# Sums of squared residuals on GpSimd, and a new order of the weight splits in the norm

## The chip, the core and the metric

The kernel runs on one core of one Trainium2 chip, as one program. The metric is the device time of one execution in microseconds (us), from its start to its end. The profile is of one execution of the same program.

## The reference

The program computes one sequence of 256 tokens with 1024 features through two blocks. The first is a Mamba-2 mixer and a convolutional feed-forward net, then an attention with dilated windows and a second such net. The second has two layers, each with a retention and convolution mixer, a cross-attention to a memory, and a gated net. What bears on the change is that every sub-layer starts with an RMS norm of the running sum x and ends by adding its output to x:

```python
def rms_norm(x, g):
    xf = x.astype(jnp.float32)
    y = xf * lax.rsqrt(jnp.mean(xf * xf, axis=-1, keepdims=True) + RMS_EPS)
    return (y * g.astype(jnp.float32)).astype(x.dtype)

# first block
x = x + _mamba2_mixer(_rms_norm(x, a_norm[i]), ...)
x = x + _conv_ffn(_rms_norm(x, ffn_norm[layer]), ...)
x = x + _dilated_mixer(_rms_norm(x, b_norm[j]), k_sh, v_sh, ...)
# second block, for each layer
u = rms_norm(h, norm_mix_g[l])
h = h + mixer_sublayer(u, ...)
h = h + memory_cross_attention(rms_norm(h, norm_xattn_g[l]), mem_n, ...)
h = h + conv_ffn(rms_norm(h, norm_ffn_g[l]), w_up[l], ...)
```

## The kernel before

Activations lie with features on the 128 partitions: x is 8 chunks of 128 features by 256 tokens. All weights are streamed from HBM as 350 units of up to 128x2048 elements, four buffers `raw` deep. Products are made to float32 accuracy from three passes in the faster fp32r format: each weight unit and each input is split into a high part and a low part, and TensorE multiplies high by high, high by low and low by high. ScalarE casts `raw` into `w_hi` (its `split`, L2054; in halves L2051 and L2052 for a few units), VectorE subtracts it to make `w_lo` (its `split`, L1191; in halves L1186 and L1188). Both have two buffers, so unit g+2 can be cast only when TensorE is done with unit g. A "feat" unit is 2 chunks of output from 8 chunks of input: 48 matmuls of 256 columns into one PSUM bank, in the order of the semaphores `hi_ready`, `lo_ready`, `unit_done`, `acc_free`.

The units form segments (`up_a`, `down`, `att_k`, ...), which all engines walk through in the same order. On each engine the order of the work is written out by hand, one instruction queue for each engine, with `project` running a segment unit by unit: split of unit u+2, `first` (what empties the bank), `second` (what has time). SyncE issues the load of a unit when `lo_ready` says that its buffer's former unit has been split.

**The end of a sub-layer** is `residual` on VectorE. For the kind "feat" (att_o, mix of both layers, mem_o of both layers; 4 units each) each unit goes: x plus the bank for two chunks (L1321), then `early_parts`, which makes the un-normalised input x times the next norm's gain and splits it (in_hi L1278, in_lo L1282), then the split of unit u+2, then in `second` two additions `ssum += sq2[m]` (L1342). The squares `sq2` are made by ScalarE (L2130, in its own `residual`) once x is ready and the former two sums are done (`sum_ready`). The other kinds (ssm_out, down) work chunk by chunk, wholly on VectorE, and aren't touched.

**The start of a sub-layer.** The first three units of the next segment (EARLY = 3) multiply the un-normalised input, so they don't wait for the norm; their banks are multiplied by 1/rms afterwards (`scale_unit`, L1197). Meanwhile TensorE sums `ssum` over the partitions with one matmul (`norm_stats`, L769). It stands behind the whole of the segment's first unit for those behind a "feat" residual and for glu of layer 0, and behind half of it otherwise. ScalarE takes the root (L2089), VectorE the reciprocal (L1368), and `norm` on VectorE makes the normalised input: eight scalings `scaled` into xn (L1375), which ScalarE casts to in_hi in four pieces (`high_parts`, L2105) and VectorE subtracts to in_lo in four pieces (`low_parts`, L1385). Unit 3 is the first to use it. `norm` also holds the splits of the segment's units 2 and 3, placed by hand. It runs seven times: ffn_a(0), attention, ffn_a(1), mixer(0), ffn_b(0), mixer(1), ffn_b(1). The cross-attention (mem_q) has its own code instead. Behind `norm`, in the two kinds of ffn, VectorE runs the convolution's taps on unit 0 (L1625, L1628), then the split of unit 4, and so on (`behind=8`); in ffn_b a product (L1680) frees the unit's bank.

**GpSimd** holds the mask of the Mamba scan, the product L2664 (up_a only) and some in_lo parts (L2654, L2697). In the attention, cross-attention and mix segments its queue was empty (`skip`).

## Time and profile before

| what | us |
|---|---|
| median of 3 runs | 2103.97 (2103.52 to 2105.73) |
| the profiled execution, device time | 2104.84 |
| its span, first to last instruction | 2103.2 |
| TensorE busy, matmuls | 2073.7 (99%) |
| VectorE busy | 1666.5 (79%) |
| ScalarE busy | 1061.2 (50%) |
| GpSimd busy | 260.0 (12%) |

The mean granted TensorE clock is 0.998 of full speed. A busy TensorE still includes short waits, since the ends of its matmuls are modelled; the start of a unit against the end of the one before shows them better. In the trace an instruction's start is followed by its duration, and where its engine stood idle before it, by that time and what ended it.

### The profile page before, as it was taken

Reading aid. Unit: us, or ns where it says so; the run is one execution under the profiler, and the core shown is the slowest. Engines: PE = TensorE matmul, PEld = TensorE weight load, DVE = VectorE, ACT = ScalarE, POOL = GpSimd, SP = SyncE. Lnnn points to the kernel's source line nnn. Section 1 sums busy time; section 2 is a strip of 40 time slices with the busy share of each in tenths; the row PEclk is TensorE's granted clock in tenths of the full one; section 3 lists DMA queues with packets and bytes.
Section 4 is the critical chain, followed back from the end, with each engine's and each line's share of the span. In section 5 each row is a group of like instructions: output and inputs, shape, how many; then the busy total and the mean of one; then the engine's idle time right before and its main releaser. Section 6 shows DMA issues by size and latency. Waiting matters only on the chain.

```text
span 2103.2 us, 40039 instructions
## 1 busy us (share of the span) xinstructions
PE 2073.7 (99%) x16378; PEld 2015.8 (96%) x16378; DVE 1666.5 (79%) x2449; ACT 1061.2 (50%) x1282; POOL 260.0 (12%) x176
## 2 busy tenths in 40 slices
PE   9999999999999999999999999999999999999998
PEld 9999999999989999989999999999988999989998
DVE  8897888788778877898986768768698996758765
ACT  6886444357754434355545445444346445445442
POOL 0212055000005500001202001100000301100100
PEclk9999999999999999999999999999999999999999
DMA  6553545453335455453554444445453555534543
GB/s 261 191 194 131 187 181 183 165 214 141 121 116 185 156 184 208 169 179 142 199 182 181 160 142 173 180 159 208 181 181 141 182 186 182 176 137 166 189 150 117
DMA packets 58281, 361.66 MB, mean 172 GB/s; under 512 B 6736, under 2 KB 9360, under 8 KB 21136
## 3 DMA queue, kind: packets, MB, share of 16 engines
q1 hardware_dynamic: 58128, 359.48, 47.9%
q8 instruction: 113, 1.85, 0.4%
q14 instruction: 40, 0.33, 0.0%
HBM read 358.37 MB, written 1.08 MB: 171 GB/s over the span
## 4 chain that ended last, share of the span: by engine, by line
PE 88%; DVE 6%; ACT 2%; issue 2%; DMA 1%; POOL 1%; SPq 0%; DVEq 0%; ACTq 0%; POOLq 0%
PE acc L639 72%; PE acc L638 7%; DVE w_lo L1191 2%; ACT w_hi L2054 1%; PE acc L754 1%; PE acc L755 1%; PE acc L756 1%; DVE arena L1413 1%; PE acc L959 1%; PE pA L1008 0%; DVE arena L1456 0%; DMA raw<-in_wide 0%; PE pB L1032 0%; PE pD L1119 0%; PE pB L1119 0%
## 5 line engine op out<-in xcount | busy, mean ns | idle before, releaser
L639 PE MATMUL acc<-in_hi,w_hi 128*128 128x256 f32 x4656 | 1306.2, 286 | 16.9 <-issue 12.1
L639 PE MATMUL acc<-in_hi,w_lo 128*128 128x256 f32 x4656 | 1292.7, 283 | 0.1
L639 PE MATMUL acc<-in_lo,w_hi 128*128 128x256 f32 x4656 | 1230.2, 283 | 0.0
L2054 ACT CAST w_hi<-raw 128x2048 fp32r<-128x2048 f32 (+1 forms) x341 | 615.4, 1805 | 667.5 <-PE acc L639 587.0
L1191 DVE TENSOR_TENSOR w_lo<-raw,w_hi 128x2048 fp32r<-128x2048 f32 (+1 forms) x341 | 738.8, 2167 | 233.2 <-ACT w_hi L2054 231.6
L639 PEld LDWEIGHTS acc<-in_hi,w_hi 128*128 128x128 f32 x4656 | 891.8, 192 | 25.8 <-issue 22.4
L639 PEld LDWEIGHTS acc<-in_hi,w_lo 128*128 128x128 f32 x4656 | 891.9, 192 | 0.6 <-DVE w_lo L1522 0.3
L639 PEld LDWEIGHTS acc<-in_lo,w_hi 128*128 128x128 f32 x4656 | 854.9, 192 | 1.2 <-issue 1.0
L2654 POOL TENSOR_TENSOR in_lo<-arena,in_hi 128x256 f32 (+2 forms) x112 | 145.2, 1296 | 1217.7 <-ACT in_hi L2514 515.7
L1835 DVE SCALAR_TENSOR_TENSOR arena<-arena,cols 128x256 f32<-128x256 f32 x480 | 200.3, 487 | 0.0
L2664 POOL TENSOR_TENSOR arena<-arena 128x256 f32<-128x256 f32 x44 | 81.9, 1861 | 387.9 <-ACT arena L2336 387.9
L2338 ACT CAST in_hi<-arena 128x256 f32 (+1 forms) x88 | 35.8, 407 | 185.8 <-POOL arena L2664 99.3
L1628 DVE SCALAR_TENSOR_TENSOR arena<-acc,cols,arena 128x255 f32<-128x255 f32 (+1 forms) x264 | 114.8, 476 | 9.2 <-DVE arena L1628 2.0
L1625 DVE TENSOR_SCALAR arena<-acc,cols 128x256 f32<-128x256 f32 x132 | 62.1, 498 | 42.3 <-PE acc L639 38.0
L638 PE MATMUL acc<-w_hi,in_hi 128*128 128x512 f32 (+1 forms) x240 | 91.0, 382 | 0.0
L638 PE MATMUL acc<-w_lo,in_hi 128*128 128x512 f32 (+1 forms) x240 | 88.2, 370 | 0.0
L638 PE MATMUL acc<-w_hi,in_lo 128*128 128x512 f32 (+1 forms) x240 | 86.1, 369 | 0.0
L638 PEld LDWEIGHTS acc<-w_hi,in_hi 128*128 128x128 f32 x240 | 45.3, 189 | 7.9 <-issue 0.5
L638 PEld LDWEIGHTS acc<-w_lo,in_hi 128*128 128x128 f32 x240 | 45.2, 188 | 7.7
L638 PEld LDWEIGHTS acc<-w_hi,in_lo 128*128 128x128 f32 x240 | 44.3, 189 | 8.0 <-issue 1.0
L754 PE MATMUL acc<-in_hi,w_hi 128*128 128x256 f32 x160 | 46.2, 289 | 0.2
L755 PE MATMUL acc<-in_lo,w_hi 128*128 128x256 f32 x160 | 45.2, 283 | 0.0
(293 smaller groups left out, 1628.1 us busy)
## 6 DMA issues: line engine op xcount, KB each, us to landing
raw<-in_wide SPq DMA_DIRECT2D x285, 1024.0 KB, 4.8
raw<-in_narrow SPq DMA_DIRECT2D x64, 704.0 KB, 4.0
arena<-cs_rows SPq DMA_DIRECT2D x16, 256.0 KB, 4.6
arena<-in_mem SPq DMA_DIRECT2D x3, 1024.0 KB, 6.9
x<-in_x SPq DMA_DIRECT2D x4, 256.0 KB, 6.5
raw<-in_wide SPq DMA_DIRECT2D x2, 512.0 KB, 5.8
tables<-in_tables SPq DMA_DIRECT2D x1, 1024.0 KB, 15.4
arena<-cs_rows SPq DMA_DIRECT2D x16, 64.0 KB, 5.3
```

The lines of the kernel that those rows point to most:

```text
L638: return mm(outs[m], moving[:, c, at], w[:, k, :], start=start, stop=stop)
L639: return mm(outs[m], w[:, k, at], moving[:, c, :], start=start, stop=stop)
L754: mm(out, hi[:, k, at], in_hi[:, c, :], start=k == 0 and m == 0, stop=False)
L755: mm(out, hi[:, k, at], in_lo[:, c, :], start=False, stop=False)
L1191: tt(w_lo[g % 2][:, 0:n], raw[g % RAW][:, 0:n], w_hi[g % 2][:, 0:n], ALU.subtract).then_inc(lo_ready, 1)
L1625: E.mark(ts(out, bank, w(2), None, ALU.mult) if bias is None else ts(out, bank, w(2), bias, ALU.mult, ALU.add))
L1628: ins = stt(out=o, in0=bank[:, 0:T - n], scalar=w(2 - n), in1=o, op0=ALU.mult, op1=ALU.add)
L1835: ins = stt(out=cvo[:, c, :], in0=src, scalar=w, in1=cvo[:, c, :], op0=ALU.mult, op1=ALU.add)
L2054: copy(w_hi[g % 2][:, 0:n], raw[g % RAW][:, 0:n]).then_inc(hi_ready, 1)
L2338: copy(in_hi[:, bass.ds(u + DC, 1), :], f_h[:, r, :].unsqueeze(1)).then_inc(inh_ready, 1)
L2654: tt(in_lo[:, d, :], src(u, j), in_hi[:, d, :], ALU.subtract).then_inc(gin_ready, 1)
L2664: tt(f_h[:, j % 2, :], f_s[:, j % 2, :], f_v[:, j % 2, :], ALU.mult).then_inc(hid_ready, 1)
```

## The change

The change has two parts. First, the two additions a unit `ssum += sq2[m]` in the five "feat" residuals leave VectorE and stand in GpSimd's queue as `residual_sums`, in the attention, mixer and cross stages; VectorE no longer waits for the last sum at the end of such a residual. Second, `norm` on VectorE makes the splits of unit 2 and unit 3 earlier: unit 2's ahead of all eight scalings, and unit 3's directly behind the scaling of unit 0's bank, with all low parts and the scaling of unit 1's bank behind it. On ScalarE the cast of unit 3 stands between the second and the third high part.

```diff
--- before.py
+++ after.py
@@ -1335,12 +1335,7 @@
                 def second(u, j, banks):
                     if beside:
                         beside(u, j, banks)
-                    if kind == "feat":
-                        E.wait(square_a)
-                        for m in range(2):
-                            dve.wait_ge(sum_ready, u * 2 + (sums + 1 + m))
-                            tt(ssum, ssum, sq2[:, m, :], ALU.add).then_inc(sum_ready, 1)
-                    elif not (isinstance(u, int) and u == last):
+                    if kind != "feat" and not (isinstance(u, int) and u == last):
                         sums_of(u, j)
 
                 def sums_of(u, j):
@@ -1356,7 +1351,8 @@
                 seg = project(name, first_and_last, second, steps={v_order: marks}, early=kind == "feat")
                 E.passed(sum_ready, 1 + DC)
                 freed(seg)
-                dve.wait_ge(sum_ready, E.seen[sum_ready])
+                if kind != "feat":
+                    dve.wait_ge(sum_ready, E.seen[sum_ready])
                 return seg
 
             def squares(src, c):
@@ -1389,13 +1385,12 @@
 
                 seg, half = take.next(), NORM_PIECES // 2
                 reciprocal_std(rstd[:])
-                scaled(name, x, rstd, xn, val_ready, range(DC // 2))
                 split(2, seg, 2)
-                scaled(name, x, rstd, xn, val_ready, range(DC // 2, DC))
+                scaled(name, x, rstd, xn, val_ready)
                 scale_unit(seg, nth, 0)
+                split(3, seg, 3)
                 low_parts(xn, chunk0, half, DC // NORM_PIECES)
                 scale_unit(seg, nth, 1)
-                split(3, seg, 3)
                 low_parts(xn, chunk0, NORM_PIECES, DC // NORM_PIECES, first=half)
 
 
@@ -2098,8 +2093,8 @@
                 E.wait(ssum_ready)
                 root(pA[:, 0:T], 1.0 / D, "eps_rms", std_ready, std[:])
 
-            def high_parts(src, chunk0, pieces, each, ready=None):
-                for n in range(pieces):
+            def high_parts(src, chunk0, pieces, each, ready=None, first=0):
+                for n in range(first, pieces):
                     if ready is not None:
                         E.wait(ready)
                     copy(in_hi[:, slots(chunk0 + n * each, each), :], src[:, n * each:(n + 1) * each, :]
@@ -2109,9 +2104,11 @@
 
                 seg = take.next()
                 roots()
+                half = NORM_PIECES // 2
                 split(2, seg, 2)
-                high_parts(xn, chunk0, NORM_PIECES, DC // NORM_PIECES, val_ready)
+                high_parts(xn, chunk0, half, DC // NORM_PIECES, val_ready)
                 split(3, seg, 3)
+                high_parts(xn, chunk0, NORM_PIECES, DC // NORM_PIECES, val_ready, first=half)
 
             def two_roots():
 
@@ -2654,6 +2651,14 @@
                     tt(in_lo[:, d, :], src(u, j), in_hi[:, d, :], ALU.subtract).then_inc(gin_ready, 1)
                 E.sweep(seg, body)
 
+            def residual_sums(nth):
+
+                for u in range(DC // 2):
+                    E.wait(square_a)
+                    for m in range(2):
+                        pool.wait_ge(sum_ready, (1 + DC) * nth + 2 * u + 1 + m)
+                        tt(ssum, ssum, sq2[:, m, :], ALU.add).then_inc(sum_ready, 1)
+
             def ffn(name, n):
                 def multiply(u, j):
 
@@ -2680,7 +2685,18 @@
                     low_parts("conv_out", piece["mix"][l], lambda u: bass.ds(u * 2 + MIX_AT, 2),
                               lambda u, j: gate[:, bass.ds(u * 2 + DC, 2), :])
                     skip("mix")
+                    residual_sums(4 + 3 * l)
                 return run
+
+            def cross(l):
+                def run():
+                    skip("mem_q", "mem_v", "mem_o")
+                    residual_sums(5 + 3 * l)
+                return run
+
+            def attention():
+                skip("att_k", "att_v", "att_q", "att_o")
+                residual_sums(2)
 
             def ssd_mask(g):
 
@@ -2697,8 +2713,8 @@
                     tt(in_lo[:, d, :], xbc[:, 2 * g:2 * g + 2, :], in_hi[:, d, :], ALU.subtract).then_inc(gin_ready, 1)
                 skip("xbc", "z", "ssm_out")
 
-            stages(mamba, ffn("up_a", 0), lambda: skip("att_k", "att_v", "att_q", "att_o"),
-                   ffn("up_a", 1), second=lambda l: (mixer(l), lambda: skip("mem_q", "mem_v", "mem_o"),
+            stages(mamba, ffn("up_a", 0), attention,
+                   ffn("up_a", 1), second=lambda l: (mixer(l), cross(l),
                                                      ffn("up_b", 2 + l)))
```

## Rows read from the trace of the kernel before

**Rows 1.** The page, busy time of each engine: us (share of the span) xinstructions.

```profile
PE 2073.7 (99%) x16378; PEld 2015.8 (96%) x16378; DVE 1666.5 (79%) x2449; ACT 1061.2 (50%) x1282; POOL 260.0 (12%) x176
```

**Rows 2.** TensorE's waits over the whole span: us in total, times, longest us.

```profile
PE acc L639 <- issue: 12.1, 25, 1.1
...
PE acc L639 <- DVE in_hi L1278: 0.2, 1, 0.2
```

**Rows 3.** Timeline, end of att_o and start of ffn_a(1): start us, duration us, what.

```profile
605.46 2.28 DVE L1191 TENSOR_TENSOR w_lo<-raw,w_hi 128x2048 fp32r<-128x2048 f32 x1
...
607.84 0.35 PE L639 MATMUL acc<-in_hi,w_hi 128*128 128x256 f32 x1 [1.99 <-ACT w_hi L2054]
...
630.89 2.28 DVE L1191 TENSOR_TENSOR w_lo<-raw,w_hi 128x2048 fp32r<-128x2048 f32 x1
...
633.34 0.28 PE L639 MATMUL acc<-in_hi,w_hi 128*128 128x256 f32 x1
```

**Rows 4.** Timeline of the norm in ffn_b(0), VectorE and TensorE.

```profile
1264.88 1.67 DVE L1375 SCALAR_TENSOR_TENSOR arena<-x,cols,rstd 128x256 f32<-128x256 f32 x4
...
1268.86 0.35 PE L639 MATMUL acc<-in_hi,w_hi 128*128 128x256 f32 x1 [0.66 <-issue]
...
1270.86 1.28 DVE L1385 TENSOR_TENSOR in_lo<-arena,in_hi 128x512 fp32r<-128x512 f32 x2
...
1275.23 0.36 PE L639 MATMUL acc<-in_hi,w_hi 128*128 128x256 f32 x1 [0.39 <-issue]
...
1279.94 0.41 DVE L1680 TENSOR_TENSOR arena<-arena,acc 128x256 f32<-128x256 f32 x1
...
1281.06 0.28 PE L639 MATMUL acc<-in_hi,w_hi 128*128 128x256 f32 x1
```

**Rows 5.** The sums (L1342) and GpSimd's product (L2664): duration ns min/median/max.

```profile
L1342 DVE TENSOR_TENSOR arena<-arena x40: 412/422/427, 597.2 to 1905.3; 128x256 f32<-128x256 f32 x40
...
L2664 POOL TENSOR_TENSOR arena<-arena x44: 728/2369/2534, 262.8 to 742.0; 128x256 f32<-128x256 f32 x44
```

**Rows 6.** Timeline in ret_g of layer 0: VectorE and GpSimd side by side.

```profile
1021.61 1.26 DVE L1835 SCALAR_TENSOR_TENSOR arena<-arena,cols 128x256 f32<-128x256 f32 x3
...
1022.79 2.28 DVE L1191 TENSOR_TENSOR w_lo<-raw,w_hi 128x2048 fp32r<-128x2048 f32 x1
1022.89 3.33 POOL L2654 TENSOR_TENSOR in_lo<-arena,in_hi 128x512 fp32r<-128x512 f32 x1 [3.08 <-ACT in_hi L2514]
1025.00 2.30 DVE L1835 SCALAR_TENSOR_TENSOR arena<-arena,cols 128x256 f32<-128x256 f32 x3
```

**Rows 7.** Timeline, mix of layer 0 (first two) and the first unit behind mem_o.

```profile
1163.11 2.28 DVE L1191 TENSOR_TENSOR w_lo<-raw,w_hi 128x2048 fp32r<-128x2048 f32 x1
...
1165.56 0.29 PE L639 MATMUL acc<-in_hi,w_hi 128*128 128x256 f32 x1
...
1258.35 2.28 DVE L1191 TENSOR_TENSOR w_lo<-raw,w_hi 128x2048 fp32r<-128x2048 f32 x1
...
1261.86 0.38 PE L769 MATMUL pA<-arena,ones 128*128 128x256 f32 x1
```

**Rows 8.** Timeline of TensorE in mixer(0): the starts of units 2 and 4.

```profile
815.68 0.36 PE L639 MATMUL acc<-in_hi,w_hi 128*128 128x256 f32 x1 [0.56 <-issue]
...
827.87 0.28 PE L639 MATMUL acc<-in_hi,w_hi 128*128 128x256 f32 x1
```

**Rows 9.** Timeline in ffn_a(0): the split of unit 4 and its start.

```profile
261.25 2.28 DVE L1191 TENSOR_TENSOR w_lo<-raw,w_hi 128x2048 fp32r<-128x2048 f32 x1
...
264.20 0.28 PE L639 MATMUL acc<-in_hi,w_hi 128*128 128x256 f32 x1
```

**Rows 10.** Timeline in the attention's norm: VectorE, and TensorE at the second att_v unit.

```profile
448.65 0.69 DVE L1197 TENSOR_TENSOR acc<-acc,rstd 128x512 f32<-128x512 f32 x1
...
454.99 2.29 DVE L1191 TENSOR_TENSOR w_lo<-raw,w_hi 128x2048 fp32r<-128x2048 f32 x1 [1.46 <-ACT w_hi L2054]
...
458.13 0.28 PE L638 MATMUL acc<-w_hi,in_hi 128*128 128x256 f32 x1
```

## Prediction, made before the changed kernel was run

> **What bounds the kernel now.** I read the page's busy shares first [rows 1]: TensorE is busy for 99% of the span, so only what makes it wait can move the time. Next TensorE's list of waits: the longest entry is 25 short idles put down to "issue" in front of the weight products (L639), 12.1 us in all [rows 2]. In the timeline, the larger ones on which this change bears stand at a unit's start, right behind the VectorE subtraction that makes w_lo (L1191): 605.46 + 2.28 = 607.74, TensorE at 607.84 [rows 3], so the signal takes 0.10 us. In such places VectorE's queue is the bound; elsewhere it runs a little ahead of TensorE. So for each site I ask how much room there is, and whether the edit uses it up. A unit takes 5.8 us on TensorE (1275.23 to 1281.06 [rows 4]).
>
> **Part 1, sums on GpSimd.** In five residuals (att_o, mix twice, mem_o twice) VectorE loses two additions a unit, 40 in all, 0.42 us each [rows 5], which is 0.79 a unit in its queue, since neighbours overlap. GpSimd gains them. Its own two-operand instruction of this size takes 0.73 us at best, but 2.37 in the median [rows 5]. The timeline says why [rows 6]: a GpSimd subtraction (512 elements) that starts 0.10 us behind an L1191 ends 1.15 us after that L1191 (1022.89 + 3.33 against 1025.07), so it waited for it. It goes the other way too: three L1835, each with two operands in SBUF, take 1.26 us together before it, and 2.30 behind the L1191, where the first was issued while GpSimd was already waiting. So the two engines take turns, the one that asks first goes first, and GpSimd waits for no more than the instruction in flight.
>
> The Trainium skill ("SBUF — State Buffer", section "Who interferes with whom") has this as a rule: a VectorE instruction with two SBUF inputs contends with a GpSimd instruction that reads SBUF, and the one that issues first holds the shared ports for its whole length. The trace agrees, by the 2.30 against 1.26 us. By the rule rival 1 can't happen; without it part 1 would come to -1.6.
>
> What is left of a 256-element addition once VectorE lets go I take as 0.6 us (0.73 less its start), and its cost to a full VectorE queue as 0.55. In the residuals VectorE's in_lo products (L1282) and its splits (L1186, L1188, L1191) all read two SBUF tiles.
> - att_o (once): VectorE is full from the second unit's split up to the next segment's first, whose L1191 ends 0.10 before TensorE starts [rows 3]. Two pairs of sums gone ahead of it save 1.6; of GpSimd's six additions that ask before it five fall between VectorE's contending instructions, 0.55 each: 2.75. The first unit of up_a comes 1.15 later. There TensorE also waited for in_hi (L1278; an idle of 0.2 in the list [rows 2], 0.4 from start to start), which goes. Net +0.7. Bounds: -1.6 with no collision, +1.7 with six and nothing absorbed.
> - mix (twice): half of unit 2's split is held up 0.55, then unit 3's split as much, less the 0.8 of the sum that is gone: it ends 0.3 later. It ended at 1165.39, and TensorE came at 1165.56 [rows 7]; with the signal 0.07 is free: +0.23. In mem_o unit 3's split is further ahead: 0.
> - the last pair of sums (mix and mem_o, four times): TensorE reads ssum (L769) behind the next segment's first unit. VectorE's last split ends at 1258.35 + 2.28 = 1260.63; two additions on GpSimd (0.6, then 0.05 and 0.74) and a signal of 0.05 give 1262.07. L769 came at 1261.86 [rows 7]: +0.2. At best 0, at worst 1.6, with one addition behind a further instruction. In att_o the last square comes well before the split: nothing more.
>
> Sum of part 1: 0.7 + 2 x 0.23 + 4 x 0.2 = +2.0 us. ScalarE's next square now waits for GpSimd, and the next w_hi cast stands behind it; it is idle there in any case, waiting for TensorE. No DMA is moved; SyncE waits for lo_ready alone. GpSimd has nothing else to do then: it is busy 12% [rows 1], and its next work is the hidden layer's, later.
>
> **Part 2, the order in norm().** Seven norms. VectorE now does split(2) ahead of all eight scalings (before, behind four), and split(3) ahead of scale_unit(1) and all four low parts (before, behind the first three of these five). ScalarE casts unit 3's w_hi behind two high parts, not four. The work is the same; what counts is what now stands behind the splits. Four scalings take 1.6 us, two low parts 1.2 (1.28 with the overlap) [rows 4], a scale_unit 0.6 (0.69 [rows 10]): so 1.8 us move behind split(3).
> - ffn_b (twice): TensorE starts units 2 and 3 at 1268.86 and 1275.23, with idles of 0.66 and 0.39 shown; against its own 5.76 us a unit it is 0.82 and 0.55 late [rows 4]. Both waits go: 1.37. But split(3) starts only 1.6 us earlier and has 1.8 more behind it, so the taps, split(4) and the multiply that frees the bank (L1680, ending 1279.94 + 0.41 = 1280.35) come 0.25 later: 1280.6, with the signal 1280.7. TensorE used to start unit 4 at 1281.06. Of the 1.37 only this is kept: -0.37 each.
> - ffn_a(1): the same, but its taps are longer, and unit 4 at 633.34 stood right behind its split (630.89 + 2.28 = 633.17) [rows 3]. It now comes 0.17 later; the two gains before it are given back: +0.17.
> - mixer(0): the same two waits (0.56 shown at 815.68), and unit 4 began at 827.87 without a wait [rows 8]. The new limit is ScalarE, whose unit-1 function waits for scale_unit(1), and which casts unit 4 after it: about 822.9 to 824.8, the split to 827.2, TensorE 827.3: -0.6.
> - ffn_a(0): here the statistics come half a unit earlier and nothing waited. split(2) still waits for a cast that hangs on TensorE, so VectorE stands idle for the 1.6 us in which it used to scale. split(3) stays where it is and all behind it comes 1.8 later: split(4) from 261.25 to 263.05, done at 265.34, with the signal 265.44, against TensorE's turn at 264.20 [rows 9]: +1.25.
> - attention: the same, and worse through ScalarE. scale_unit(1) moves from 448.65 to 452.85; ScalarE's three copies of unit 1 wait for it, and the cast of the fifth unit stands behind them in its queue: it ends at 457.2 instead of 454.9. The split at 454.99, which had waited 1.46 for that cast, ends at 459.6 instead of 457.28; TensorE's turn was 458.13 [rows 10]: +1.6 at most, 1.2 if every signal is as short as it can be. I take +1.4.
> - mixer(1): as ffn_a(0), but there unit 4 has more room: +0.1.
>
> Sum of part 2: -0.74 + 0.17 - 0.6 + 1.25 + 1.4 + 0.1 = +1.6. Bounds: -0.5 with each late chain 0.4 shorter, +3 with each 0.2 longer.
>
> **The sum.** 2.0 + 1.6 = +3.6, say 3.5 us. The profiled execution took 2104.84 us, 2103.2 of span and 1.6 around it; the median of the runs is 2103.97, 0.9 below. Against the median: 2107.5. The shifts last to the end, since later waits hang on TensorE's own units.
>
> **Rivals.**
> 1. *No collisions.* att_o gives -1.6, mix and the last sums 0: with part 2 all told 0: 2104. Rows 6 speak against it.
> 2. *The waits at units 2 and 3 are gained for good* in the four norms that have them, and the early norms lose nothing: -5.5, with part 1's +2.0 it is -3.5: 2100.5, and with rival 1 2097. It needs unit 4 not to be next; rows 3 and 4 say that it is.
> 3. *GpSimd loses its turn (slower).* Where VectorE's instructions touch (in_hi, in_lo, split in a row), an addition that asks while one runs may be passed by the next, and so wait for the split's end. Then the last square waits for the sum before it, and L769 comes 1.4 to 1.6 us later than forecast, in each of mix and mem_o: +6 on top: 2113. It decides from the first addition that is passed by a second instruction; rows 6 show one that was not.
> 4. *Attention's chain is longer (slower):* the late cast also delays the scaling for b_norm and what follows in att_q: 1 to 3 us more, 2109.5.
>
> **How the numbers follow.** The forecast's case has 0.60 (2105 to 2109.5), rival 1 0.13, rival 2 0.07, rival 3 0.10, rival 4 0.10. A change under 0.2%, 4.2 us, can't be told from none: slower begins at 2108.2, faster at 2099.8. Of the forecast's 0.60 a quarter, 0.15, lies above 2108.2. Slower: 0.15 + 0.10 and most of rival 4, 0.07: 0.32. Faster: nearly all of rival 2: 0.06. Same: 0.62. For 8 in 10 the range goes from 2101.5 (part of rival 2 left out) to 2111 (rival 3 left out).
>
> **What would show it.** Right: in the five residuals GpSimd additions of 0.74 us beside others of 1 to 2.5; up_a(1)'s first unit about 1 us later; a wait of 0.2 of L769 for GpSimd; no wait at units 2 and 3 in ffn_b and a new one at unit 4; in attention a new idle of 1 to 1.6 in front of the second att_v unit, and in ffn_a(0) one of about 1 in front of unit 4. Wrong: additions of 0.74 throughout (rival 1), unit 4 on time (rival 2), L769 waiting over 1 us (rival 3), new idles in att_q (rival 4).

## The result, and the profile after

The changed kernel takes 2108.95 us in the median of 15 runs (2107.47 to 2110.83), the kernel before 2103.97 (2103.29 to 2105.85, 15 runs beside them). The ratio is 1.0023, interval 1.0016 to 1.0031: about 5 us slower. The forecast was 2107.5, range 2101.5 to 2111.0. The median lies above 2108.2, where the prediction lets slower begin (0.2%), but the lower end of the interval, 1.0016, is under that line. The profiled execution of the changed kernel has a span of 2107.6 us, 4.4 more than the profile of before.

The page of the changed kernel: busy time of each engine, and the group of the sums now on GpSimd (busy us, mean ns of one | idle before).

```profile
PE 2076.0 (98%) x16378; PEld 2017.3 (96%) x16378; DVE 1652.8 (78%) x2409; ACT 1060.0 (50%) x1282; POOL 320.2 (15%) x216
...
L2660 POOL TENSOR_TENSOR arena<-arena 128x256 f32<-128x256 f32 x40 | 60.2, 1504 | 396.6 <-ACT arena L2127 395.0
```

VectorE is busy 13.7 us less and GpSimd 60.2 us more [rows 1]; forty additions that VectorE did in 0.42 us each [rows 5] take 1.50 us on average on GpSimd. TensorE's busy time grew by 2.3 us with the same number of instructions, which the prediction had no term for.

TensorE's list of waits after (us in total, times, longest):

```profile
PE acc L639 <- issue: 10.3, 19, 1.2
PE acc L639 <- ACT w_hi L2049: 2.9, 1, 2.9
...
PE acc L638 <- issue: 1.7, 1, 1.7
PE acc L639 <- DVE arena L1675: 1.5, 2, 0.7
```

Against [rows 2] the idles put down to "issue" in front of L639 went from 12.1 us (25) to 10.3 (19): the eight waits at units 2 and 3 of four norms are gone, and two are new, 1.1 and 1.2 us in front of unit 4 of ffn_a(0) and ffn_a(1). The idle of 2.9 us in front of ffn_a(1)'s first unit is the one of 1.99 in [rows 3], now longer. Two more entries are new: one of 1.7 in front of the second att_v unit (L638), and two in front of unit 4 of ffn_b, on L1675, the product that frees the bank. In ffn_a(0) it is this row:

```profile
264.54 0.36 PE L639 MATMUL acc<-in_hi,w_hi 128*128 128x256 f32 x1 [1.14 <-issue]
```

**How the places are compared.** In the timelines of two kernels I read the start of each unit's first matmul and take the difference. Behind the first 17 units and ssm_out, told below, it stays constant from unit to unit within 0.1 us except at a few places. Each jump belongs to one edit or to TensorE's clock at ffn_a(1), but for three of 0.3 to 0.4 us in experiments (at 893 us in three norms, without and with feeding, and at 1537 us in sums alone) whose cause is open. In us, a plus is later:

| place | forecast | after | in the experiments |
|---|---|---|---|
| att_o, up to ffn_a(1)'s first unit | +1.15 | +0.95 | sums alone +0.96; no reads -1.31; att_o on VectorE 0 |
| the same, by its second unit | -0.4 | +0.99 | sums alone +0.92; norms alone +1.02; no reads -0.48; fed -0.48 |
| mix, twice | +0.46 | 0 and +0.14 | no reads 0 |
| last sums, four times | +0.8 | +0.32, +0.32, +0.34, +0.33 | no reads 0 |
| ffn_b, twice | -0.74 | -0.35, -0.36 | norms alone -0.32, -0.31 |
| ffn_a(1)'s norm | +0.17 | +0.12 | norms alone +0.16 |
| mixer(0) | -0.6 | -0.57 | norms alone -0.55 |
| ffn_a(0) | +1.25 | +1.30 | norms alone +1.31 |
| attention | +1.4 | +1.83 | norms alone +1.84; scaling first +0.36 |
| mixer(1) | +0.1 | +0.14 | norms alone +0.16 |
| sum | +3.6 | +5.5 | |

The forecast column holds the prediction's terms. Beside these places the first 17 units (mamba), whose code is unchanged, are 0.9 us shorter in the profile of after; in the other profiles they are 0.3 to 1.6 shorter than in the profile of before. So the profiled spans differ by 4.4 where the edits account for 5.5, and the medians by 5.0.

Timeline of the changed kernel at the end of att_o, answering to [rows 3] (start us, duration us, what, idle in front):

```profile
606.92 1.36 DVE L1282 SCALAR_TENSOR_TENSOR in_lo<-x,cols,in_hi 128x256 fp32r<-128x256 f32 x2
...
607.08 1.79 POOL L2660 TENSOR_TENSOR arena<-arena 128x256 f32<-128x256 f32 x2 [0.86 <-ACT arena L2127]
...
608.20 2.81 DVE L1191 TENSOR_TENSOR w_lo<-raw,w_hi 128x2048 fp32r<-128x2048 f32 x1
...
611.11 0.55 PE L639 MATMUL acc<-in_hi,w_hi 128*128 128x256 f32 x1 [2.94 <-ACT w_hi L2049]
```

The GpSimd pair of additions (L2660) asks about 0.15 us behind the start of VectorE's pair of products (L1282). That pair takes 1.36 us instead of 0.88, and the L1191 that meets the second addition 2.81 instead of 2.28. The split ends at 611.01 and TensorE starts at 611.11, as the prediction reads it. What it did not foresee is in the next view: busy time by stretch and, third from the right, the clock that TensorE was granted, for 2.9 us ahead of that first unit, 3.4 us in it, and 3.4 us behind.

```profile
core 0: us, PE busy (x) PEld busy (x) DVE busy (x) ACT busy (x) POOL busy (x), PEclk, DMA share, GB/s
608.20:611.10 2.90, 0.00 (x0) 0.02 (x1) 2.90 (x3) 1.90 (x1) 0.66 (x1) 0.99 0.00 0
611.10:614.50 3.40, 3.39 (x16) 3.40 (x17) 3.29 (x7) 2.12 (x3) 1.71 (x2) 0.51 0.63 236
614.50:617.90 3.40, 3.40 (x30) 3.40 (x30) 1.91 (x1) 0.00 (x0) 0.00 (x0) 1.00 0.33 99
```

In the unit's first 3.4 us the granted clock is 0.51, the level of 1.2 GHz; behind them it is 1.0, 2.4 GHz. TensorE issues 16 matmuls in that stretch, 30 in the next. Kernel before, the same two places (2.0 us of idle, then 3.4 us of the first unit):

```profile
605.80:607.80 2.00, 0.05 (x1) 0.00 (x0) 2.00 (x2) 1.86 (x1) 0.00 (x0) 1.00 0.01 4
607.80:611.20 3.40, 3.14 (x24) 2.97 (x25) 3.26 (x9) 1.94 (x3) 0.00 (x0) 1.00 0.73 231
```

There it stayed at 1.0. The Trainium skill has the rule in "TensorE: Matmul & The Clock Gate", Part 1 (The HAM clock gate): TensorE runs at half its clock when it has not been busy lately. By that rule the trace agrees, in the 0.51 behind 2.9 us of idle. It is not the whole account: the last section has a place where the clock fell with no such idle ahead of it.

The last sums, in ffn_b(0) behind mem_o, answering to [rows 7]:

```profile
1262.59 2.28 DVE L1191 TENSOR_TENSOR w_lo<-raw,w_hi 128x2048 fp32r<-128x2048 f32 x1
...
1262.98 3.30 POOL L2660 TENSOR_TENSOR arena<-arena 128x256 f32<-128x256 f32 x2 [2.44 <-ACT arena L2127]
...
1266.34 0.70 PE L769 MATMUL pA<-arena,ones 128*128 128x256 f32 x2
```

VectorE's L1191 ends at 1264.87, the GpSimd pair at 1266.28, 1.41 later (forecast: 0.6 + 0.05 + 0.74 = 1.39), and L769 starts 0.06 behind it.

The norm in ffn_b(0), answering to [rows 4]: three splits, the starts of units 2, 3 and 4, and the product that frees the bank.

```profile
1269.44 2.29 DVE L1191 TENSOR_TENSOR w_lo<-raw,w_hi 128x2048 fp32r<-128x2048 f32 x1
...
1272.62 0.28 PE L639 MATMUL acc<-in_hi,w_hi 128*128 128x256 f32 x1
...
1275.82 2.29 DVE L1191 TENSOR_TENSOR w_lo<-raw,w_hi 128x2048 fp32r<-128x2048 f32 x1 [0.31 <-ACT w_hi L2049]
...
1278.38 0.28 PE L639 MATMUL acc<-in_hi,w_hi 128*128 128x256 f32 x1
...
1282.52 2.28 DVE L1191 TENSOR_TENSOR w_lo<-raw,w_hi 128x2048 fp32r<-128x2048 f32 x1
1284.72 0.41 DVE L1675 TENSOR_TENSOR arena<-arena,acc 128x256 f32<-128x256 f32 x1
...
1285.28 0.35 PE L639 MATMUL acc<-in_hi,w_hi 128*128 128x256 f32 x1 [0.74 <-DVE arena L1675]
```

Units 2 and 3 start without idle, 120 ns behind the matmul ahead of them; unit 4 waits 0.74 for L1675, which ends at 1285.13.

### The profile page after: what moved, and what is told of

Read it like the earlier page. It is cut to its first block, busy times and chain, and to the rows that moved or that the text cites. A ratio compares the mean times of both kernels' runs of the same rounds, so it can differ in the third digit from the quotient of the medians.

```text
span 2107.6 us, 40046 instructions
## 1 busy us (share of the span) xinstructions
PE 2076.0 (98%) x16378; PEld 2017.3 (96%) x16378; DVE 1652.8 (78%) x2409; ACT 1060.0 (50%) x1282; POOL 320.2 (15%) x216
## 4 chain that ended last, share of the span: by engine, by line
PE 87%; DVE 5%; ACT 3%; issue 3%; POOL 1%; DMA 1%; SPq 0%; DVEq 0%; ACTq 0%; POOLq 0%
PE acc L639 70%; PE acc L638 7%; ACT w_hi L2049 2%; DVE w_lo L1191 2%; PE acc L754 1%; PE acc L755 1%; PE acc L756 1%; PE acc L959 1%; POOL arena L2660 1%; PE pA L1008 0%; DVE arena L1371 0%; PE pB L1032 0%; DVE in_lo L1381 0%; PE pD L1119 0%; PE pB L1094 0%
## 5 line engine op out<-in xcount | busy, mean ns | idle before, releaser
L639 PE MATMUL acc<-in_hi,w_hi 128*128 128x256 f32 x4656 | 1307.7, 286 | 17.2 <-issue 10.3
L639 PE MATMUL acc<-in_hi,w_lo 128*128 128x256 f32 x4656 | 1293.8, 283 | 0.1
L639 PE MATMUL acc<-in_lo,w_hi 128*128 128x256 f32 x4656 | 1231.4, 283 | 0.1
L1191 DVE TENSOR_TENSOR w_lo<-raw,w_hi 128x2048 fp32r<-128x2048 f32 (+1 forms) x341 | 741.0, 2173 | 238.2 <-ACT w_hi L2049 237.0
L639 PEld LDWEIGHTS acc<-in_hi,w_hi 128*128 128x128 f32 x4656 | 893.1, 192 | 25.8 <-issue 19.8
L639 PEld LDWEIGHTS acc<-in_hi,w_lo 128*128 128x128 f32 x4656 | 893.0, 192 | 0.6 <-DVE w_lo L1517 0.3
L639 PEld LDWEIGHTS acc<-in_lo,w_hi 128*128 128x128 f32 x4656 | 855.1, 192 | 2.1 <-issue 1.0
L2660 POOL TENSOR_TENSOR arena<-arena 128x256 f32<-128x256 f32 x40 | 60.2, 1504 | 396.6 <-ACT arena L2127 395.0
L2669 POOL TENSOR_TENSOR arena<-arena 128x256 f32<-128x256 f32 x44 | 81.9, 1861 | 154.1 <-ACT arena L2333 154.1
L638 PE MATMUL acc<-w_hi,in_hi 128*128 128x512 f32 (+1 forms) x240 | 91.1, 382 | 1.7 <-issue 1.7
L638 PE MATMUL acc<-w_lo,in_hi 128*128 128x512 f32 (+1 forms) x240 | 88.1, 370 | 0.0
L638 PE MATMUL acc<-w_hi,in_lo 128*128 128x512 f32 (+1 forms) x240 | 86.2, 369 | 0.0
L638 PEld LDWEIGHTS acc<-w_hi,in_hi 128*128 128x128 f32 x240 | 45.3, 189 | 9.7 <-issue 2.3
L638 PEld LDWEIGHTS acc<-w_lo,in_hi 128*128 128x128 f32 x240 | 45.2, 188 | 7.7
L638 PEld LDWEIGHTS acc<-w_hi,in_lo 128*128 128x128 f32 x240 | 44.3, 189 | 8.0 <-issue 1.0
```

The lines of the kernel that those rows point to most:

```text
L638: return mm(outs[m], moving[:, c, at], w[:, k, :], start=start, stop=stop)
L639: return mm(outs[m], w[:, k, at], moving[:, c, :], start=start, stop=stop)
L1191: tt(w_lo[g % 2][:, 0:n], raw[g % RAW][:, 0:n], w_hi[g % 2][:, 0:n], ALU.subtract).then_inc(lo_ready, 1)
L2660: tt(ssum, ssum, sq2[:, m, :], ALU.add).then_inc(sum_ready, 1)
L2669: tt(f_h[:, j % 2, :], f_s[:, j % 2, :], f_v[:, j % 2, :], ALU.mult).then_inc(hid_ready, 1)
```

## The experiments

Ratios are to the kernel before, run on the same chip beside each.

| kernel | median us | before us | ratio | interval |
|---|---|---|---|---|
| sums alone | 2107.48 | 2104.49 | 1.0014 | 1.0005 to 1.0023 |
| norms alone | 2107.20 | 2104.49 | 1.0012 | 1.0003 to 1.0021 |
| three norms | 2103.80 | 2104.49 | 0.9996 | 0.9987 to 1.0005 |
| no reads | 2104.68 | 2104.49 | 1.0001 | 0.9992 to 1.0011 |
| att_o on VectorE | 2108.19 | 2104.46 | 1.0018 | 1.0009 to 1.0027 |
| scaling first | 2107.22 | 2104.46 | 1.0012 | 1.0003 to 1.0022 |
| changed kernel, fed | 2108.18 | 2104.46 | 1.0018 | 1.0008 to 1.0027 |
| three norms, fed | 2102.94 | 2104.46 | 0.9992 | 0.9983 to 1.0001 |
| before, fed | 2103.83 | 2104.71 | 0.9996 | 0.9987 to 1.0005 |
| high parts on ScalarE | 2102.66 | 2104.71 | 0.9991 | 0.9981 to 1.0000 |

The theory from the prediction: GpSimd and VectorE take turns at their reads (part 1), and what stands behind the splits in VectorE's queue sets the later units (part 2). The rivals: GpSimd's extra work or its longer signals cost by themselves; the norms' gains are for good.

**1. Sums alone**: the changed kernel, with norm() and ScalarE's order put back.

```diff
-                scaled(name, x, rstd, xn, val_ready)
+                scaled(name, x, rstd, xn, val_ready, range(DC // 2))
+                split(2, seg, 2)
+                scaled(name, x, rstd, xn, val_ready, range(DC // 2, DC))
```

> Part 1 alone: sums on GpSimd, the norm's order as before. Theory (the two parts add up, and the sums cost through collisions between GpSimd and VectorE): in the changed kernel's trace the steps at the residuals are +1.9 us at att_o and 0.3 to 0.5 at each of mix and mem_o, 3.4 together, so 1.0016 of the time before (+3.4 us, 2.4 to 4.4), the units of up_a(1) starting 1.9 us late against the unit before att_o. Rival (the loss at att_o comes from the new order of the norm): +1.5 us or less, att_o's step under 0.5.

**2. Norms alone**: the changed kernel, with the additions back on VectorE in all five residuals.

```diff
+                    if kind == "feat":
+                        E.wait(square_a)
+                        for m in range(2):
+                            dve.wait_ge(sum_ready, u * 2 + (sums + 1 + m))
+                            tt(ssum, ssum, sq2[:, m, :], ALU.add).then_inc(sum_ready, 1)
```

> Part 2 alone: the norm's new order, sums on VectorE. Theory: +1.3 us in ffn_a(0), +1.8 in attention, +0.1 in each of ffn_a(1) and mixer(1), -0.6 in mixer(0), -0.35 in each ffn_b: +2.1 us (1.0010; 1 to 3). Rival (the new order gains, and the sums eat it): -2 us or more below the kernel before, no new wait in front of the second att_v unit.

Measured, 1 and 2: 3.0 and 2.7 us above the kernel before, together 5.7, where both parts at once give 5.0. The profiles of both hold the low clock at ffn_a(1), 1.4 and 1.0 us, which the changed kernel has once. So the parts add up within the noise, and neither gains. But their split is not the forecast's: each of them has a jump of about one microsecond at ffn_a(1)'s second unit (+0.92 and +1.02), and with the norms alone nothing was changed there. In the profile of the norms alone, the first 3.4 us of that first unit:

```profile
610.20:613.60 3.40, 3.39 (x17) 3.40 (x18) 3.26 (x9) 1.93 (x3) 0.00 (x0) 0.54 0.65 219
```

A granted clock of 0.54, behind an idle of 2.0 us, where the kernel before has 1.0 behind the same idle.

**3. Three norms**: sums on VectorE, new order in mixer(0) and the two ffn_b only, where the prediction's terms are negative.

```diff
+                if nth in (3, 5, 8):
+                    split(2, seg, 2)
+                    scaled(name, x, rstd, xn, val_ready)
+                    scale_unit(seg, nth, 0)
+                    split(3, seg, 3)
```

> The new order only in mixer(0) and the two ffn_b, the old one in the other four norms, sums on VectorE. Theory (each norm is decided by its own slack): -0.6 - 2 x 0.35 = -1.3 us, 0.9994, and unit 4 of up_b starting 0.35 us earlier against unit 1 than before. Rival (the two waits that go are kept in full): -1.37 x 3 = -4.1 us.

Measured: the three places give -0.55, -0.33 and -0.34, 1.2 us together; the median is 0.7 below the kernel before (expected: 1.3), and the interval includes no difference. The low clock came here too, at ffn_a(1) (the unit's start and what follows) and once more in ssm_out, which may be where the rest went:

```profile
608.10:611.50 3.40, 3.27 (x19) 2.99 (x20) 3.26 (x9) 1.95 (x3) 0.00 (x0) 0.71 0.68 241
611.50:614.90 3.40, 3.40 (x25) 3.40 (x25) 2.41 (x3) 0.16 (x1) 0.00 (x0) 0.79 0.37 108
```

**4. No reads**: the changed kernel with GpSimd's additions replaced by instructions that read nothing. Its sum of squares is the constant 1, so the normalised values are not the reference's.

```diff
-                        tt(ssum, ssum, sq2[:, m, :], ALU.add).then_inc(sum_ready, 1)
+                        nc.gpsimd.memset(ssum, 1.0).then_inc(sum_ready, 1)
```

> The changed kernel with each of GpSimd's 40 additions replaced by a GpSimd memset of ssum to one: the sum is left out, all waits and signals between ScalarE, GpSimd, VectorE and TensorE stay. Theory (VectorE is held up because GpSimd reads SBUF): VectorE's L1282 pairs at att_o take 0.88 us again instead of 1.36, its splits 2.28 instead of 2.8, up_a(1)'s first unit starts over 2.5 us earlier than in the changed kernel, the time falls by 3 us or more below the changed kernel's. Rival (the chain of signals through GpSimd, with ScalarE's square waiting for it and its w_hi casts behind): durations may shorten, but the time falls by under 1 us.

Measured: 0.2 us above the kernel before, with an interval that includes no difference, where the changed kernel is 5.0 above: 4.8 less. The end of att_o:

```profile
604.99 0.87 DVE L1282 SCALAR_TENSOR_TENSOR in_lo<-x,cols,in_hi 128x256 fp32r<-128x256 f32 x2
...
605.27 0.68 POOL L2660 MEMSET arena<- 128x256 f32 x2 [1.64 <-ACT arena L2127]
...
605.78 2.28 DVE L1191 TENSOR_TENSOR w_lo<-raw,w_hi 128x2048 fp32r<-128x2048 f32 x1
...
608.17 0.36 PE L639 MATMUL acc<-in_hi,w_hi 128*128 128x256 f32 x1 [0.68 <-issue]
```

GpSimd's pair again starts in the middle of VectorE's L1282, with the same waits and signals, but now L1282 takes 0.87 and L1191 2.28 us, as before the change, and TensorE starts 1.31 us earlier than before instead of 0.95 later: 2.26 us for collisions and slower additions together (expected: over 2.5). The pair of fills is also shorter (0.68 us against 1.8), but it overlaps VectorE's pair and leaves nothing of the delay: so it is the reads that cost. The four jumps of +0.33 at the last sums are gone too. This kernel's TensorE is idle for only 0.7 us there, and its clock stays at 1.0. The rule in the Trainium skill, "SBUF — State Buffer", section "Who interferes with whom", has this very case: VectorE with two SBUF inputs contends with GpSimd instructions that read SBUF, not with those that only write it. The trace agrees, by 2.81 against 2.28 us.

**5. att_o on VectorE**: the changed kernel with att_o's additions back on VectorE, the other four residuals' on GpSimd.

```diff
+                    if kind == "feat" and nth == 2:
+                        E.wait(square_a)
+                        for m in range(2):
+                            dve.wait_ge(sum_ready, u * 2 + (sums + 1 + m))
+                            tt(ssum, ssum, sq2[:, m, :], ALU.add).then_inc(sum_ready, 1)
```

> The changed kernel with the additions of att_o's squares back on VectorE (the other four places stay on GpSimd). Theory: the part of the loss at att_o that comes from the two engines reading at once is undone: ffn_a(1)'s first unit starts 0.9 to 1.0 us earlier than in the changed kernel (its step against the kernel before goes from +0.95 to 0), VectorE's products at in_lo go back from 1.36 to 0.88 us and its last split from 2.8 to 2.3. The second half of that loss, the +0.99 that the first unit's own length added, stays in part: in two runs without GpSimd's additions it was there too (+1.02, +1.29), with a granted clock of 0.5 after the idle time. So 2107.0 to 2108.2 with the low clock, 2106.0 to 2107.0 without. Rival (all of the +1.94 comes from the additions on GpSimd, and the clock with it): 2106.0 to 2107.0, never a low clock. The four +0.32 steps in mem_q and ffn_b stay by both.

Measured: no jump at the first unit nor at the second; VectorE's L1282 and L1191 are back at 0.88 and 2.28 us:

```profile
607.02 0.88 DVE L1282 SCALAR_TENSOR_TENSOR in_lo<-x,cols,in_hi 128x256 fp32r<-128x256 f32 x2
607.81 2.28 DVE L1191 TENSOR_TENSOR w_lo<-raw,w_hi 128x2048 fp32r<-128x2048 f32 x1
```

In this profile the clock stayed at 1.0 behind an idle of 2.0 us (the unit's first 3.4 us):

```profile
610.20:613.60 3.40, 3.18 (x24) 2.98 (x25) 3.26 (x9) 1.94 (x4) 0.00 (x0) 1.00 0.70 231
```

So the first half of the loss at att_o is GpSimd's. The median, 3.7 us above the kernel before, is at the upper end of what was expected with a low clock; one profile at 1.0 does not say how many of the ten runs had it. The rival "never a low clock" is neither shown nor excluded by it.

**6. Scaling first**: in attention's norm VectorE scales the second early unit's result ahead of the fourth unit's split. The changed kernel there, first: VectorE's scaling, ScalarE's first function on it and its next cast, VectorE's split, TensorE.

```profile
453.33 0.69 DVE L1197 TENSOR_TENSOR acc<-acc,rstd 128x512 f32<-128x512 f32 x1
...
454.13 0.60 ACT L2398 ACTIVATE arena<-acc 128x512 f32<-128x512 f32 x1 [1.50 <-DVE acc L1197]
...
455.99 1.91 ACT L2049 CAST w_hi<-raw 128x2048 fp32r<-128x2048 f32 x1
...
458.00 2.29 DVE L1191 TENSOR_TENSOR w_lo<-raw,w_hi 128x2048 fp32r<-128x2048 f32 x1 [2.18 <-ACT w_hi L2049]
...
460.39 0.36 PE L638 MATMUL acc<-w_hi,in_hi 128*128 128x256 f32 x1 [1.67 <-issue]
```

```diff
                 scale_unit(seg, nth, 0)
+                if nth == 1:
+                    scale_unit(seg, nth, 1)
                 split(3, seg, 3)
```

> The changed kernel with one step of attention's norm moved: VectorE's scaled weights of the second early unit (scale_unit(1)) come ahead of the split of the fourth unit's weights, everywhere else as changed. Theory 1: the +1.83 in attention is the fourth unit's split standing in VectorE's queue ahead of the scaled weights that TensorE's second early unit and ScalarE's cast wait for; moved, the second unit's wait goes, and the step at att_v falls to between 0 and +0.5: about 1.5 us under the changed kernel, 2107.4. Theory 2: it comes from ScalarE's order (two copies of the normalised input behind the cast of the fourth unit's weights); then VectorE's order doesn't matter, the step stays above +1.3, and the time stays at 2108.5 to 2109.

Measured: the jump in attention falls from +1.83 to +0.36, as theory 1 had it:

```profile
449.35 1.29 DVE L1197 TENSOR_TENSOR acc<-acc,rstd 128x512 f32<-128x512 f32 x2
450.55 2.28 DVE L1191 TENSOR_TENSOR w_lo<-raw,w_hi 128x2048 fp32r<-128x2048 f32 x1
...
454.96 1.91 ACT L2052 CAST w_hi<-raw 128x2048 fp32r<-128x2048 f32 x1
...
456.96 2.29 DVE L1191 TENSOR_TENSOR w_lo<-raw,w_hi 128x2048 fp32r<-128x2048 f32 x1 [1.12 <-ACT w_hi L2052]
...
459.36 0.36 PE L638 MATMUL acc<-w_hi,in_hi 128*128 128x256 f32 x1 [0.20 <-issue]
```

Both scalings run in one go at 449.35. The cast now starts at 454.96 rather than 455.99, though all of this kernel runs 0.44 later up to here, and TensorE idles 0.20 instead of 1.67. The +0.36 that is left is ScalarE's own order: its three functions of that unit come behind two copies of the normalised input (1.14 us), which before stood ahead of the fourth unit's cast. They delay the next cast by 1.1 us, and 0.75 of that was free ahead of TensorE's turn. So theory 2 has a fifth of it.

The time, 2107.22, is near the 2107.4 of theory 1, but partly by chance: the ten executions fall into two groups. Four have a mean granted clock of 0.999 and take 2106.1 to 2106.4 us, six have 0.998 or less and take 2106.8 to 2108.7; the profile is of the second group. A stretch of 3.4 us at half the clock lowers the mean by 0.0008, so the first four probably passed ffn_a(1) at full clock, in spite of an idle that should be as long.

**7 to 9. Feeding TensorE.** Nine matmuls of ones (overwritten by the unit's own first product) in TensorE's idle time ahead of ffn_a(1)'s first unit: in the changed kernel (7), in three norms (8), in the kernel before (9).

```diff
+                    if g == 92:
+                        pe.wait_ge(acc_free, u + (seg.base - 3))
+                        warm(9, unit_bank(seg, j))
```

> The changed kernel with nine matmuls of ones (128 by 128, fp32, their result is overwritten) put on TensorE in its idle time ahead of ffn_a(1)'s first unit, once its bank is free. They end before that unit's weights are split, if each takes 0.2 to 0.25 us. Theory (the clock fell because TensorE stood idle for 2 to 3 us): the granted clock stays 1.0 through the first unit, that unit takes 5.7 to 6.2 us instead of 7.18, and the time is 1.0 to 1.4 us under the changed kernel, 2107.6 to 2108.0. Rival (the clock falls whatever TensorE does there, for the chip's own reasons, or the unit's length comes from a wait): length and time stay as in the changed kernel.

> The kernel before with the new order in three norms alone (mixer(0) and the two ffn_b: two thirds of a microsecond for two of them and 0.6 for the first in earlier runs) and the same nine matmuls ahead of ffn_a(1)'s first unit. Theory: minus 0.57 minus 2 times 0.35 is minus 1.3, and no low clock there, which in the kernel before comes in some executions only and costs 1.0 to 1.3 us when it does: 2101.8 to 2102.8, ratio 0.9990 to 0.9995. Rival (the matmuls delay the first unit, or the low clock comes elsewhere instead): 2103.0 to 2104.0, no difference from the kernel before.

> The kernel before with nothing but the nine matmuls of ones on TensorE ahead of ffn_a(1)'s first unit, behind the wait for its bank. In the kernel before TensorE stands idle there for 2.0 us (its last matmul of att_o ends at 605.8, the next begins at 607.84), and in profiles with that same idle time the granted clock fell to 0.5 in two (the norms alone, three norms) and stayed at 1.0 in two (before, att_o's sums on VectorE). Theory: the kernel before loses 1.0 to 1.3 us in a part of its executions, so that feeding TensorE there gives nothing in the fastest and 0.3 to 0.8 us in the median: 2103.4 to 2104.2 beside 2104.4, ratio 0.9996 to 0.9999, and the first unit at 1.0. Rival (in the kernel before the clock nearly always falls there, and the profile of it was the exception): 1.0 us or more, 2103.2 or less.

Measured: in the changed kernel the first unit takes 5.71 us instead of 7.18, from the start of its first matmul to the start of its last. The stretch with the nine matmuls, then the unit's first 3.4 us:

```profile
608.00:611.00 3.00, 2.05 (x20) 1.89 (x18) 3.00 (x3) 1.90 (x1) 0.74 (x1) 1.00 0.00 0
611.00:614.40 3.40, 3.40 (x28) 3.40 (x29) 3.29 (x7) 2.12 (x3) 1.73 (x2) 1.00 0.71 241
```

28 matmuls in 3.4 us instead of 16, at a clock of 1.0. The time, 2108.18, is 0.2 above the expected 2107.6 to 2108.0; against the kernel before beside it, it is 3.7 above where the changed kernel is 5.0 above: 1.3 less. Over all profiles: with TensorE idle for 2.9 us ahead of this unit (after, sums alone, scaling first) the clock fell in three of three; with 2.0 us (before, norms alone, three norms, att_o on VectorE) in two of four; where it was idle for less than 1.0 us (no reads, and the four kernels with the nine matmuls) in none of five. Three norms, fed, takes 2102.94, 1.5 below the kernel before; that is 0.14 above what the theory allowed and just under the rival's 2103.0. Its first unit has a clock of 1.0 (from 606.5 to 609.9 us), and its three norms gain 0.56, 0.34 and 0.34 us. It is faster than the changed kernel beyond doubt (their intervals to the kernel before lie apart) and likely faster than the kernel before, but the interval of 0.9983 to 1.0001 just includes no difference. The kernel before, fed, takes 2103.83, 0.9 below the kernel before, between theory (0.3 to 0.8) and rival (1.0), with an interval that includes no difference. How often the kernel before has the low clock at this place stays open. There is one hint: none of its 87 executions in these experiments has a mean granted clock of 0.999, and 17 of the 42 executions of kernels with the nine matmuls have.

**10. High parts on ScalarE**: experiment 8, and in att_o the early high parts made by ScalarE; VectorE's additions move behind the next addition to x.

```diff
+                    if name == "att_o":
+                        for c in (2 * u, 2 * u + 1):
+                            fn(in_hi[:, LATE_AT + c:LATE_AT + c + 1, :], x[:, c:c + 1, :], ACT.Copy,
+                               scale=wcol("ffn_norm1", c)).then_inc(early_hi, 1)
```

> The new order in three norms and the nine matmuls, as in the kernel of 2102.9 us, and in att_o alone the early high parts (x times its column, 0.62 us a unit on VectorE) made by ScalarE as two copies with a scale, ahead of its square; on VectorE a unit's two additions move behind the next unit's addition to x, so that they stand in its queue while ScalarE makes the high parts. Theory (VectorE's queue sets the end of att_o; ScalarE has time to spare there, 6.95 of 14 us busy, and does not share VectorE's way to memory as GpSimd does): VectorE is relieved of 0.54 us a unit, ffn_a(1)'s first unit starts 0.8 to 1.3 us sooner than in the kernel of three norms, and VectorE's durations stay as they are (0.88 for a pair, 2.28 for a split): 2101.4 to 2102.4, ratio 0.9985 to 0.9991. Rival (ScalarE's later square and cast are waited for, or its reads lengthen VectorE's work as GpSimd's did): 2102.9 to 2103.6.

Measured: 2102.66 (2101.91 to 2103.87, but for one execution of 11448 us), between the theory's 2102.4 and the rival's 2102.9; against the kernel before beside each it is 2.1 us down, experiment 8 1.5, and the intervals overlap. So the time doesn't decide, but the trace does. ScalarE's cast, then two rows of VectorE:

```profile
596.89 1.03 ACT L2069 CAST w_hi<-raw 128x1024 fp32r<-128x1024 f32 x1
...
597.95 1.23 DVE L1189 TENSOR_TENSOR w_lo<-raw,w_hi 128x1024 fp32r<-128x1024 f32 x1 [0.88 <-ACT w_hi L2069]
...
604.84 0.88 DVE L1285 SCALAR_TENSOR_TENSOR in_lo<-x,cols,in_hi 128x256 fp32r<-128x256 f32 x2 [0.79 <-ACT in_hi L2156]
```

ScalarE's two copies push its cast back (596.89, where experiment 8 has 595.09 in a kernel that is 1.0 us ahead there), and VectorE, relieved of 0.54 us a unit, stands idle for 0.88 us for that cast and 0.79 for the high parts. ffn_a(1)'s first unit comes 0.54 later than in the kernel before and its second 0.49 sooner again. VectorE's durations did not grow beside ScalarE's reads (0.88, 1.23). The rival's first half was right (ScalarE's later cast is waited for), its second half not: the bound there is the chain through both engines, not VectorE's queue alone.

## Why the prediction was right, and where it was not

- *What bounds*: the reading of [rows 3], of VectorE's split with TensorE 0.10 behind it, holds in all twelve profiles, and six of the ten lines of the table came out within 0.2 us.
- *Collisions* [rows 6]: right in mechanism and nearly in size. Up to the split's end VectorE's instructions grew by 0.48 three times, 0.54 and 0.53, 2.51 us for five additions; the prediction had 5 x 0.55 = 2.75. Less the 1.6 of sums gone: +0.9, measured +0.95. Experiment 4 shows that the reads are the cause. Rival 1 is out.
- *The term of att_o was mis-sized*, +0.7 against +1.94. The wait for in_hi went as forecast (-0.48 in experiments 4 and 7, forecast -0.4). What was missing is TensorE's clock: idle for 2.9 us instead of 2.0, TensorE began the unit at half its clock, and the unit was 7.18 us long against 5.71 with feeding, 1.47 us lost. 0.95 - 0.48 + 1.47 = 1.94. Without the clock the term would have been +0.47. The prediction treated a longer idle as costing its length only.
- *Attention*: +1.83 against +1.4, above the bound of 1.6. The mechanism is shown by experiment 6. The chain is that of the text (scaling at 453.33, three functions of ScalarE, cast, split), all of it 0.43 later in this profile; the cast then ends 0.26 later than forecast, since the scaling takes 0.69 and not 0.6 and its signal and the functions' order a little more.
- *mix*: forecast +0.23 twice, measured 0 and +0.14, and the mechanism was wrong in part. The addition that asks during the first half of unit 2's split (L1186) did not hold up the second half: L1188 keeps its 1.22 us and goes first, and the GpSimd pair takes 3.30. What the second addition of that pair held up is an instruction that the prediction had at nothing, L1278, which reads one SBUF tile and a column: a single one takes 0.80 us instead of 0.35, the pair 1.06 instead of 0.62. With 0.79 of sums gone and 0.44 for this, unit 3's split stands 0.35 earlier. In layer 0 it then runs unhindered, and the jump is 0. In layer 1 it takes 2.83 and ends 0.19 later, and the jump is +0.14; sums alone and att_o on VectorE, where it takes 2.28, have no jump there.

```profile
1162.27 3.30 POOL L2660 TENSOR_TENSOR arena<-arena 128x256 f32<-128x256 f32 x2 [4.76 <-ACT arena L2127]
...
1164.92 1.06 DVE L1278 TENSOR_SCALAR in_hi<-x,cols 128x256 fp32r<-128x256 f32 x2
...
1811.51 2.83 DVE L1191 TENSOR_TENSOR w_lo<-raw,w_hi 128x2048 fp32r<-128x2048 f32 x1
```

- *Last sums*: +0.33 each against +0.2. The pair ended within 0.02 of the forecast; behind the wait L769 and the matmuls after it start up more slowly (L769 +0.23, the next unit +0.32). Rival 3 did not occur there: the four pairs take 3.30 to 3.31 us, and L769 follows.
- *Rival 3's mechanism exists*, though, four times in the profile of after: at the first unit of both mix, as just told, and at the second unit of mix in layer 0 and mem_o in layer 1 (first additions of 3.07 and 3.00 us). Nothing waits for these:

```profile
1165.90 0.87 DVE L1282 SCALAR_TENSOR_TENSOR in_lo<-x,cols,in_hi 128x256 fp32r<-128x256 f32 x2
...
1166.50 3.89 POOL L2660 TENSOR_TENSOR arena<-arena 128x256 f32<-128x256 f32 x2 [0.93 <-ACT arena L2127]
...
1166.70 2.28 DVE L1191 TENSOR_TENSOR w_lo<-raw,w_hi 128x2048 fp32r<-128x2048 f32 x1
```

  The addition asks at 1166.50, in the second half of VectorE's pair (ends 1166.77), and L1191, which is queued right behind, runs its full 2.28 us ahead of it. So an addition can be passed by a second instruction, against the prediction's reading of [rows 6] that it waits for no more than the one in flight. At the second unit of mix in layer 1 an addition that asks just as late (0.20 us into VectorE's product) went first and held up the split; what decides is open. The 0.10 of the prediction was the chance that this happens at the last sums.
- *Norms*: ffn_b -0.36 (-0.37), ffn_a(1) +0.12 (+0.17), mixer(0) -0.57 (-0.6), ffn_a(0) +1.30 (+1.25), mixer(1) +0.14 (+0.1). As forecast, what units 2 and 3 gain (0.82 + 0.61) unit 4 gives back, in ffn_b 1.07 and in ffn_a(1) 1.56 of 1.44. Rival 2 is out.
- *The total*: edits of +5.5 against +3.6. Of the 1.9 missing, 1.2 is att_o (its clock costs 1.5), 0.4 attention, 0.5 the last sums, less 0.3 in mix. The median is 1.45 us above the forecast. It is inside the range because the range was made wide for the rivals; no term or rival of the prediction had the clock, the largest single miss.
- *Reading the profile of before*: its first 17 units happened to be the slowest of all profiles by 0.3 to 1.6 us; a single span can't be held against a median to better than that.

## What to carry to other kernels

Before moving work to GpSimd, look at what VectorE runs beside it. Where that reads two SBUF tiles, a GpSimd addition of 0.74 us cost VectorE 0.5, more than the 0.42 it saved; L1278, with one tile and a column, lost 0.44. L1321, which reads a PSUM bank and one tile, lost nothing beside 13 additions. When an operation is moved ahead in a queue, follow the resource that the last unit of the group needs: here units 2 and 3 gained 1.4 us and unit 4 paid them back, and the only lasting gains (0.3 to 0.6 us) were where it had room. And a longer TensorE idle can cost more than its length: ask whether the clock falls behind it, and if so, a few dummy matmuls in that idle time can give back as much as a good reordering (1.3 us here). Look at the granted clock of several executions: one profile shows one case.

## What the runs showed of the hardware

At ffn_a(1)'s first unit the granted clock of TensorE fell to the level of 1.2 GHz behind a single idle of 2.9 us in three of three profiles, and of 2.0 us in two of four, in a kernel whose TensorE is otherwise 99% busy; with nine small matmuls in the idle it stayed at 2.4 GHz in four of four. The cost was 1.0 to 1.5 us each time, and it shows at a unit that no edit touches. The clock also falls in ssm_out, from 193 us on, in four of the profiles (three norms, att_o on VectorE, before fed, high parts on ScalarE), here in the kernel before, fed:

```profile
189.00:193.00 4.00, 3.82 (x34) 3.64 (x32) 2.00 (x6) 2.58 (x3) 0.00 (x0) 1.00 0.00 0
193.00:197.00 4.00, 4.00 (x22) 4.00 (x22) 3.98 (x7) 1.01 (x2) 0.47 (x1) 0.57 0.19 39
```

There TensorE had stood idle for no more than 0.2 us at a time in the 16 us ahead; so a long idle isn't needed for a fall, and what brings this one about is open. A wait at the next unit, which in the kernel before is one of 0.7 us for a GpSimd in_lo, takes up most of the loss: against where each profile stood, ssm_out's second unit starts 1.1 to 1.2 us later than in the kernel before and the third 0.2 to 0.5.

A GpSimd addition of two tiles that asks 0.15 us behind a VectorE instruction with two SBUF inputs made VectorE's pair of products 0.48 us longer and its long split 0.53, though the addition itself takes 0.73 us when alone. Of two VectorE instructions with a single SBUF tile one was held up by GpSimd's additions and one was not: L1278 (a tile times a column) took 0.79 to 0.80 us instead of 0.35 in four of four places in the profile of after, L1321 (a PSUM bank plus a tile) stayed at 0.41 to 0.43 in 13 of 13. Beside the fills of experiment 4 no L1278 takes over 0.36.
